# An RWKV and mixture-of-experts kernel: GpSimd's third receptance remainder waits for the low parts of the mixed input, and VectorE's own second one goes ahead of them

## The reference

```python
xx = jnp.pad(h, ((0, 0), (1, 0), (0, 0)))[:, :-1] - h
xs = h[None] + xx[None] * mu[:, None, None, :]
rkv = jnp.einsum('pbtd,pde->pbte', xs[:3], w_rkv)
r, k, v = rkv[0], rkv[1], rkv[2]
```

## Time and profile before

| | before |
|---|---|
| median of 3 runs | 1187.51 us |
| lowest and highest run | 1185.41 and 1188.8 us |
| span of the profiled execution | 1188.3 us |
| TensorE matmul busy | 1058.0 us (89%) |
| VectorE, ScalarE, GpSimd busy | 481.0, 473.2, 461.2 us |
| mean granted TensorE clock | 0.945 |

### The profile page before, as it was taken

The page is one execution under the profiler, slowest core; times in us unless marked ns, Lnnn a source line. Parts: engine busy times, 40 slices in busy tenths (PEclk is TensorE's granted clock), DMA queues, the critical chain, the costliest instruction groups (busy, mean ns, idle before and its releaser), DMA issues.

```text
span 1188.3 us, 22136 instructions
## 1 busy us (share of the span) xinstructions
PE 1058.0 (89%) x9609; PEld 897.8 (76%) x9622; DVE 481.0 (40%) x720; ACT 473.2 (40%) x638; POOL 461.2 (39%) x106
## 2 busy tenths in 40 slices
PE   6999999999999898999999999999999885555555
PEld 5899889999989888889878988998978553333333
DVE  2052331011036566442346886887342642121213
ACT  5454455445466652223154434445552321111112
POOL 4878748878861223402162434443653000000000
PEclk9999999999999888999999999998999898877787
DMA  9755565565543440000219788877536659999994
GB/s 362 233 175 184 177 188 168 185 199 172 193 142 109 143 155 6 3 4 7 70 71 365 256 317 320 327 266 254 171 107 252 265 221 420 421 421 422 422 421 188
DMA packets 99129, 260.93 MB, mean 220 GB/s; under 512 B 6368, under 2 KB 61024, under 8 KB 83184
## 3 DMA queue, kind: packets, MB, share of 16 engines
q1 hardware_dynamic: 93728, 249.78, 57.2%
q10 hardware_dynamic: 5328, 10.09, 2.5%
HBM read 258.80 MB, written 1.05 MB: 219 GB/s over the span
## 4 chain that ended last, share of the span: by engine, by line
PE 61%; DMA 13%; issue 13%; POOL 4%; DVE 4%; ACT 3%; SPq 1%; POOLq 0%; DVEq 0%; ACTq 0%
PE ps L1888 13%; PE ps L1890 13%; PE ps L1889 13%; DMA w_e<-in_w_expert_up 13%; POOL wlo L581 4%; PE ps L2643 4%; PE ps L2250 2%; PE ps L2259 2%; PE ps L1966 1%; PE ps L2263 1%; SPq L516 1%; PE ps L2358 1%; PE ps L2065 1%; DMA raw<-in_sgu_w_in 1%; PE ps L2175 1%
## 5 line engine op out<-in xcount | busy, mean ns | idle before, releaser
L581 POOL TENSOR_TENSOR wlo<-raw,whi 128x2048 fp32r<-128x2048 f32 x93 | 438.3, 4726 | 414.0 <-ACT whi L632 407.8
L1888 PE MATMUL ps<-Hh,whi 128*128 128x256 f32 x832 | 240.8, 289 | 8.9 <-POOL wlo L581 5.7
L632 ACT ACTIVATE whi<-raw 128x2048 fp32r<-128x2048 f32 x116 | 220.3, 1911 | 65.1 <-DMA raw<-in_ffn_w 40.2
L1890 PE MATMUL ps<-Hh,wlo 128*128 128x256 f32 x832 | 238.3, 286 | 0.0
L1889 PE MATMUL ps<-Hl,whi 128*128 128x256 f32 x832 | 238.2, 286 | 0.0
L1888 PEld LDWEIGHTS ps<-Hh,whi 128*128 128x128 f32 x832 | 162.8, 196 | 13.1 <-POOL wlo L581 11.2
L1889 PEld LDWEIGHTS ps<-Hl,whi 128*128 128x128 f32 x832 | 162.7, 196 | 0.8 <-issue 0.2
L1890 PEld LDWEIGHTS ps<-Hh,wlo 128*128 128x128 f32 x832 | 162.5, 195 | 0.0
L2643 PE MATMUL ps<-w_e,arena 128*32 128x256 f32 x896 | 74.6, 468 | 73.1 <-DMA w_e<-in_w_expert_up 69.1
L2643 PEld LDWEIGHTS ps<-w_e,arena 128*32 128x32 f32 x896 | 36.7, 134 | 104.4 <-DMA w_e<-in_w_expert_up 72.4
L1888 PE MATMUL ps<-whi,Fh 128*128 128x512 f32 x256 | 99.8, 390 | 0.0
(11 more groups left out here) (392 smaller groups left out, 1733.8 us busy)
## 6 DMA issues: line engine op xcount, KB each, us to landing
raw<-in_ffn_w SPq DMA_DIRECT2D x64, 1024.0 KB, 5.5
w_e<-in_w_expert_up SPq DMA_DIRECT2D x32, 1024.0 KB, 18.1
w_e<-in_w_expert_down SPq DMA_DIRECT2D x32, 1024.0 KB, 18.5
arena<-in_w_ada SPq DMA_DIRECT2D x24, 1024.0 KB, 11.9
w_e<-in_w_expert_gate SPq DMA_DIRECT2D x24, 1024.0 KB, 23.3
raw<-in_sgu_w_in SPq DMA_DIRECT2D x16, 1024.0 KB, 6.5
raw<-in_rwkv_w_rkv SPq DMA_DIRECT2D x12, 1024.0 KB, 5.2
raw<-in_sgu_w_out SPq DMA_DIRECT2D x8, 1024.0 KB, 4.8
```

What stands on the lines that cost most here:

```text
L581: pool.tensor_tensor(wlo[n % RING][:, :], raw[n % RING][:, :], whi[n % RING][:, :].bitcast(F32), ALU.subtract).then_inc(lo_done, 1)
L632: act.activation(whi[n % RING][:, :], raw[n % RING][:, :], ACT.Copy).then_inc(hi_done, 1)
L1888: pe.matmul(o, sh, mh, start=start, stop=False, skip_group_check=True)
L1890: return pe.matmul(o, sl, mh, start=False, stop=stop, skip_group_check=True)
```

## The change

GpSimd waits for eight counts of `xs_low`, that is for all four quarters of the receptance input's low part, before it makes the remainder of MIX+6. VectorE makes the remainder of MIX+5 before `low(1)` and no longer behind it. Nothing else is touched; the instructions that compute are the same ones.

```diff
@@ -587,6 +587,8 @@
                 for n in range(RING):
                     lo(n, i)
             for n in range(MIX, MIX_OUT, 2):
+                if n == MIX + 6:
+                    pool.wait_ge(sem("xs_low"), 8)
                 lo(n)
             pool.wait_ge(used, FIRST["rwkv_o"])
             for ap, odd in ((r_X, 1), (r_Y, 0)):
@@ -1301,8 +1303,8 @@
                                               ALU.mult, ALU.add))
                 settle()
                 dve.tensor_tensor(slot(5), slot(6), slot(5), ALU.subtract).then_inc(sem("cum_excl"), 1)
+                weight_low(MIX + 5)
                 low(1)
-                weight_low(MIX + 5)
                 dve.wait_ge(sem("xs_low"), 8)
                 mix(2, 2)
                 weight_low(MIX + 7)
```

## The result

| | before | after |
|---|---|---|
| median of 11 runs each | 1187.36 us | 1181.48 us |
| lowest to highest | 1185.41 to 1194.59 | 1179.75 to 1184.79 |
| span of the profiled execution | 1188.3 us | 1179.7 us |
| mean granted TensorE clock | 0.945 | 0.952 |

The medians differ by 5.9 us. The ratio of the two times is 0.9944 with a 95% interval from 0.9927 to 0.9961, so even its upper end is 0.39% faster, beyond the 0.3% that was set as the bound. A second comparison further down gives 4.2 us, and the upper end of its interval is only 0.2% faster. Of all the executions in this document one was in a slow state, 1218.82 us in the experiment with the longest wait, and its ratio leaves it out. The page after: TensorE's share of the chain is the same, and the others moved by a point at most.

A forecast was written before the change was run, and what follows sets the result against it. TensorE, 61% of the chain, was taken as the bound, idling before the first receptance piece. Removing the 3.24 us stall and 2.8 us of low clock gives -6.0: 1188.3 - 6.0 = 1182.3 us, range 1179.8 to 1185.8.

The forecast's parts named there:

- The stall and its cause: Before the first receptance matmul: TensorE's 3.24 us idle goes once low(1)'s first quarter no longer stands behind GpSimd's MIX+6.
- The sum: Stall and first receptance piece on TensorE: 11.86 us becomes 5.85, together -6.0 us.
- the term for the clock: First receptance piece: the low clock after the idle time goes, 8.62 us becomes 5.85, 2.8 us gained.
- The second case of the prediction: Rival: only the stall goes, since some executions may lack the clock's fall; 1184.3 us, range 1183.5 to 1185.5, chance 0.22.
- The argument ahead of that case: In the trace, 3.00 us idle preceded a low clock, 2.10 us none; 3.24 is just above, so the fall may vary.
- What queues behind GpSimd's wait: MIX+6's remainder there at 401.9, TensorE asking at 411.1; MIX+10's load also in time; cost nothing.
- The collision with mix(2): GpSimd's MIX+6 and VectorE's mix(2) wake on the same count; one waits for the other; cost 0, keeping +1 us.
- second branch: mix(2) waits for GpSimd and ends at 405.2, MIX+7 at 407.5; the norm stays ahead of TensorE.
- MIX+5 moved ahead: VectorE makes MIX+5's remainder in idle time, 388.0 to 390.3, without delaying low(1); cost nothing.
- the prediction's near miss: At the norm, L1310 just misses and waits for GpSimd's MIX+8; L1312 ends at 414.7, still 2.2 us ahead.
- Whether the gain lasts: After 411.26 every release runs through TensorE, so the gain moves along; 0 to 1.5 us given back, taken as 0.
- Slower by starvation: Rival: VectorE's two-input instructions keep GpSimd out of MIX+6 until the norm is done; about 1192 us, chance 0.04.

The follow-up runs named there:

- A second comparison: The changed kernel itself measured again against the kernel before: 1183.94 us over 12 runs, ratio 0.9962 (0.9944 to 0.9980).
- the experiment with the longest wait: Changed kernel with GpSimd making MIX+6's remainder only after VectorE has made MIX+9's: 1194.39 us, ratio to before 1.0073 (1.0038 to 1.0108).
- the five-count run: Changed kernel with GpSimd waiting for five counts of xs_low instead of eight before MIX+6: 1191.03 us, ratio to before 1.0023 (0.9998 to 1.0049).
- the run with zeros: Kernel before, with 14 TensorE matmuls on zeros ahead of the first receptance piece: 1185.46 us, ratio 0.9981 (0.9966 to 0.9995).
- three experiments: Kernel before with GpSimd's wait alone, 1182.61 us; changed kernel with GpSimd waiting for mix(2), 1181.29; changed kernel with a wait before MIX+10, 1182.88.

## Why the prediction was right

- **The stall and its cause: right.** 3.24 us went, the quarters of `low(1)` are at 0.68 us, the fourth was there in time. With a wait that ends three quarters too early (the five-count run) the stall is back on another quarter; the other half of the change without the wait leaves it in place.
- **The sum: right for the profiled execution, a little high for the typical one.** 6.0 us predicted, 6.17 in the pair of profiles. But the term for the clock, 2.8 us, was that of one execution. In three profiles of the kernel before the piece took 2.9, 1.7 and 0.2 us longer than the 5.69 of after, 1.6 on the mean, and the run with zeros recovers 2.4 us of the median (0.6 to 4.0 by its interval). The same change measured 5.9 us in the first comparison and 4.2 in the second, around 3.24 + 1.6 = 4.9. So the term was nearly twice its mean, and that the first comparison came out so close to 6.0 is partly luck. The second case of the prediction (only the stall goes) was not another outcome but what some of the executions behind a median do; it had been right to let it hold the forecast at 1182.3 instead of 1181.5. The argument ahead of that case, from one idle stretch of 3.00 us with a low clock behind it and one of 2.10 without, gave the right doubt and no size.
- **What queues behind GpSimd's wait: right.** MIX+6 came at 396.40 + 4.61 = 401.0, TensorE asked at 410.
- **The collision with mix(2): right, second branch.** GpSimd won and `mix(2)` ended at 404.1; cost nothing. In three profiles of the changed kernel VectorE began 0.04 to 0.05 us ahead of GpSimd and still stood, while with 0.16 us of lead it kept GpSimd out in three experiments. Its instructions differ too (128x256 with the short lead, 128x2048 with the long one), so that the lead decides is not shown.
- **MIX+5 moved ahead: right, cost nothing; needed: no.** The wait alone measured 5.3 us, which its interval does not tell from the changed kernel's. With it the norm came at 414.84, as the prediction's near miss has it (414.7).
- **Whether the gain lasts: right within the noise.** ScalarE's square root waited 6.53 us for TensorE; after, the same row has 0.35 us (L821), still no lateness. What was missed is small: with the clock high through the spreading, TensorE came to the value product 0.29 us before VectorE's `low(2)`, held up by L1322's meeting with MIX+10.
- **Slower by starvation: not what happened, and the price of such a wait was right.** It took an edit that holds GpSimd off until TensorE idles 9.38 us to show it. In the changed kernel VectorE did not keep GpSimd from MIX+6 at all (4.61 us), and with the wait alone by 2 us (6.56).

## What to carry to other kernels

One long instruction of an idle-time helper can hold up the short instruction that everybody waits for: look in a tile's list for a maximum far above the median, and then at what the neighbour engine ran beside it. Let the helper start behind the short one, by a wait on the last count that matters, after working out how long its own result has cover; a wait that ended three quarters early gave nothing back here. Count a low clock behind an idle stretch as a chance, not as a term, until several profiles of the same kernel have shown it.

## What the hardware showed that was not expected

An idle stretch of TensorE of one and the same length, 3.24 us, was followed by 48 matmuls in 8.62, 7.40 and 5.91 us in three executions of one kernel, at a mean granted clock of 0.64, 0.77 and 1.00. And a VectorE instruction with a single SBUF input of 16 x 256 elements (L1312, 0.28 us) took 4.71 us beside GpSimd's remainder in one kernel and 1.76 us in another, ending each time 0.14 to 0.15 us after GpSimd (413.07 against 412.92, 406.41 against 406.27). So not only the instructions with two inputs collide with it. The reciprocal of the same tile took its 1.74 us in the changed kernel although GpSimd's MIX+8 began in its midst (406.94).
